# Reordering one tile's mixer: both channel halves of four projections ahead of the long convolution, the channel norm split by token half

## What is computed

```python
def mixer_block(u, ...):
    z = u @ w_in                                   # u = rms_norm(x)
    b_a, c_a, h_a, v_b, g_b = split(z)             # 512 channels each
    y_a = b_a * causal_dwconv(c_a * h_a, conv_a_w)             # 3 taps
    glu = v_b * sigmoid(g_b)
    cb = causal_dwconv(glu, conv_b_w) + conv_b_bias            # 31 taps
    y_b = silu(layer_norm(cb, ln_b_g, ln_b_b))                 # norm over 512 channels
    return concat([y_a, y_b]) @ w_out
for l in range(2):
    h = h + mixer_block(rms_norm(h), ...)
    h = h + memory_cross_attention(rms_norm(h), rms_norm(mem), ...)   # 4 heads, 256 memory tokens
    h = h + relu(rms_norm(h) @ w_up) ** 2 @ w_down                    # width 4096
return rms_norm(h)
```

## Time and profile before

| what | value |
|---|---|
| median of 3 runs | 3471.89 us (3469.18 to 3646.47) |
| the profiled execution | 3468.78 us, of which the span of the slowest core is 3467.2 us |
| spans of the eight cores | 3442.4 to 3467.2 us, granted clock 0.981 to 0.987 |
| busy share of the span | PE 94%, DVE 51%, ACT 40%, POOL 19% |
| PE idle ahead of L450 matmuls | 126.3 us |
| PE idle ahead of L906 matmuls | 58.9 us |

### The profile page before, as it was taken

How to read it: one execution, slowest core, us unless ns; L and a number is a source line. 1 busy time by engine, 2 the same in 40 slices (tenths; PEclk the granted TensorE clock), 3 DMA queues, 4 the chain that set the end, 5 groups by cost and what they waited for, 6 DMA issues and landing times.

```text
span 3467.2 us, 50455 instructions; the slowest of 8 cores (3442.4 to 3467.2 us)
## 1 busy us (share of the span) xinstructions
PE 3257.5 (94%) x16080; PEld 1550.2 (45%) x16080; DVE 1762.9 (51%) x2912; ACT 1402.1 (40%) x2627; POOL 643.7 (19%) x884
## 2 busy tenths in 40 slices
PE   2879999999998999989998999999999899999997
PEld 0445444444454444544444444444445444454443
DVE  4846333663357532564347743376335753366433
ACT  3336322463325531464333732256333553146421
POOL 0413001320032100330004200222003210042000
PEclk9989999999999999999999999999999999999999
DMA  7686944544555444535548344344456444453441
GB/s 202 150 187 102 166 73 85 118 91 79 110 167 124 80 78 82 122 79 86 98 94 228 64 80 76 91 113 83 77 117 177 111 80 79 75 127 72 77 80 52
DMA packets 132275, 366.93 MB, mean 106 GB/s; under 512 B 13872, under 2 KB 39728, under 8 KB 132016
## 3 DMA queue, kind: packets, MB, share of 16 engines
q0 software_dynamic: 59648, 213.94, 36.5%
q1 hardware_dynamic: 63152, 145.56, 13.3%
q10 hardware_dynamic: 9216, 4.20, 0.5%
HBM read 521.98 MB, written 34.60 MB: 161 GB/s over the span
## 4 chain that ended last, share of the span: by engine, by line
PE 83%; DVE 4%; issue 4%; DMA 3%; ACT 3%; POOL 1%; SPq 1%; DVEq 0%; ACTq 0%; POOLq 0%
PE ps L450 81%; ACT arena L461 3%; DMA arena<-wts 2%; DVE arena L465 2%; PE ps L906 2%; DVE arena L475 1%; DMA wbf<-arena 1%; SPq L577 1%; POOL arena L465 1%; DVE arena L610 0%; POOL arena L479 0%; POOL arena L470 0%; POOL arena L766 0%; DVE arena L951 0%; SPq L589 0%
## 5 line engine op out<-in xcount | busy, mean ns | idle before, releaser
L450 PE MATMUL ps<-arena 128*128 128x512 bf16 (+2 forms) x15816 | 3182.7, 364 | 126.3 <-ACT arena L461 64.9
L450 PEld LDWEIGHTS ps<-arena 128*128 128x128 bf16 x15816 | 1520.8, 98 | 1785.8 <-issue 175.6
L461 ACT ACTIVATE arena<-arena 128x512 bf16<-128x512 f32 (+3 forms) x1249 | 740.6, 642 | 1265.2 <-DVE arena L465 949.3
L465 DVE TENSOR_TENSOR arena<-arena 128x512 bf16<-128x512 f32 (+3 forms) x1200 | 849.5, 715 | 653.6 <-ACT arena L461 632.2
L465 DVE TENSOR_TENSOR arena<-ps,arena 128x512 f32<-128x512 f32 (+1 forms) x448 | 303.2, 688 | 633.7 <-PE ps L450 594.4
L461 ACT ACTIVATE arena<-ps 128x512 f32<-128x512 f32 (+1 forms) x608 | 361.8, 595 | 623.0 <-PE ps L450 599.2
L416 POOL DMA_DIRECT2D arena<-wts x400 | 214.7, 538 | 1662.6 <-PE ps L450 1621.1
L465 POOL TENSOR_TENSOR arena<-arena 128x512 f32<-128x512 f32 (+1 forms) x144 | 206.7, 1439 | 609.3 <-ACT arena L461 366.0
L461 ACT ACTIVATE arena<-ps,arena 128x256 f32<-128x256 f32 (+2 forms) x441 | 228.6, 533 | 135.9 <-DVE arena L471 72.9
L465 DVE TENSOR_TENSOR arena<-arena,ps 128x512 f32<-128x512 f32 x256 | 172.8, 686 | 141.2 <-PE ps L906 81.6
L475 DVE SCALAR_TENSOR_TENSOR arena<-arena 128x384 f32<-128x384 f32 (+3 forms) x336 | 179.3, 586 | 92.0 <-ACT arena L461 91.5
(11 more groups left out here) (14 smaller groups left out, 96.9 us busy)
## 6 DMA issues: line engine op xcount, KB each, us to landing
arena<-wts POOLq DMA_DIRECT2D x400, 512.0 KB, 5.9
arena<-wbf SPq DMA_DIRECT2D x64, 576.0 KB, 4.0
arena<-wbf SPq DMA_DIRECT2D x64, 512.0 KB, 5.4
arena<-xT SPq DMA_DIRECT2D x32, 512.0 KB, 6.8
outT<-arena SPq DMA_DIRECT2D x8, 2048.0 KB, 7.1
arena<-xT SPq DMA_DIRECT2D x6, 2048.0 KB, 15.6
wbf<-arena SPq DMA_DIRECT2D x16, 576.0 KB, 3.7
arena<-arena SPq DMA_DIRECT2D x128, 64.0 KB, 3.5
```

The lines of the kernel that those rows point to most:

```text
L450: ins = e.matmul(ps.ap, lhsT=l_, rhs=r_, start=(first and i == 0), stop=(last and i == n - 1))
L461: return e.activation(**kw)
L465: S.op(eng, lambda e: e.tensor_tensor(out=out.ap, in0=a.ap, in1=b.ap, op=op), reads=[a, b], writes=[out])
```

## The change

1. Order in `mixer`: g and v of channel half 0, c and h of half 0, g and v of half 1, layout transfers of `glu`, c and h of half 1, the convolution, then all eight b groups, token half by token half. `cva` has eight buffers instead of four. The weight order `seq` follows.
2. The channel norm runs per token half: for each s, DVE subtractions and multiplications of 4 x 128 columns (none on POOL now), four Silu of 128 columns per block, and per block again two transfers from SP and two from ACT, now of 256 bytes per row instead of 512. So there are 32 Silu of 128 columns, and 32 transfers, per mixer, instead of 16 of 256 columns, and 16 transfers.
3. `await_ln(s)` replaces `finish_tasks()` at the end of the mixer: the code goes on to `attend` and asks for half s of the norm where it is read. `out_half` takes six output blocks instead of four and goes block by block, y_a inputs first.
4. `next_ps` rotates over seven banks, `next_aux` has one.
5. Strided regions are given to the scheduler piece by piece (`ivs`), so that the two token halves of `ycat`, `cb` and `yb` don't wait for each other.
6. `conv_a`'s copy of the history into `c` is issued by POOL ahead of the h group.
7. The last tile's final norm is written out in pieces of two channel blocks (`final_last`).

```diff
@@ Buf
     def r3(self, j0, j1, a=0, b=None):
...
-        return self.ref(ap, j0 * self.stride + a, (j1 - 1) * self.stride + b)
+        return self.refs(ap, [(j * self.stride + a, j * self.stride + b) for j in range(j0, j1)])
...
-        cva = [alloc(T, F32, TAU) for _ in range(4)]
+        cva = [alloc(T, F32, TAU) for _ in range(8)]
...
         def next_ps():
-            return psref(rot("ps", range(6)))
+            return psref(rot("ps", range(7)))
         def next_aux():
-            return psref(6 + rot("aux", range(2)))
+            return psref(7)
...
                 for jp in range(2):
-                    seq += [w_id(l, C_G + jp), w_id(l, C_V + jp)]
-                seq += [w_id(l, C_C), w_id(l, C_H)]
+                    seq += [w_id(l, C_G + jp), w_id(l, C_V + jp), w_id(l, C_C + jp), w_id(l, C_H + jp)]
                 seq += [b_id(l, W_CONV + i) for i in range(8)]
-                seq += [w_id(l, C_B), w_id(l, C_C + 1), w_id(l, C_H + 1), w_id(l, C_B + 1)]
+                seq += [w_id(l, C_B), w_id(l, C_B + 1)]
@@ mixer
+            gv_part(0)
+            ch_part(0)
+            gv_part(1)
             touch(AF.Ln)
             copy("pool", glc.r3(0, NG, 0, HM), gluh[l].r3(0, NG))
...
+            ch_part(1)
...
+                        c = rot("chb", chb)
+                        hh = chh[l].r(2 * j, 2 * j + 2)
+                        h3 = Ref(hh.ap.unsqueeze(2), "sb", hh.lo, hh.hi)
                         psc = grp(sc, jj, xg, s)
                         t = tmp()
                         tt("dve", t.r(), psc, RB[s].r(), ALU.mult)
+                        copy("pool", c.r3(2, 4, 0, 1), h3)
                         psh = grp(sh, jj, xg, s)
-                        c = rot("chb", chb)
                         tt("dve", c.r3(0, 4, 1, TAU + 1), ps4(psh), p4(t), ALU.mult)
-                        spawn(conv_a(s, j, c, cva[s * 2 + jj]))
+                        copy("pool", h3, c.r3(2, 4, TAU, TAU + 1))
+                        spawn(conv_a(s, j, c, cva[s * 4 + j]))
@@ ln_task
-                yield
-                for a in range(5):
-                    if a < 4:
-                        blk = cb.r3(4 * a, 4 * a + 4)
-                        tt("dve", blk, blk, bc(ln_m), ALU.subtract)
-                        tt("pool" if a % 2 else "dve", blk, blk, bc(ln_v), ALU.mult)
-                    if a > 0:
-                        silu_out(a - 1)
+                for s in range(NS):
+                    blks = [cb.r3(4 * a, 4 * a + 4, s * TAU, (s + 1) * TAU) for a in range(4)]
+                    for a in range(2):
+                        tt("dve", blks[a], blks[a], bc(ln_m, s), ALU.subtract)
                     yield
+                    for a in range(4):
+                        if a < 2:
+                            tt("dve", blks[a + 2], blks[a + 2], bc(ln_m, s), ALU.subtract)
+                        tt("dve", blks[a], blks[a], bc(ln_v, s), ALU.mult)
+                        silu_out(a, s)
+                        yield
+                    ln_done.add(s)
                     yield
                 touch(AF.Ln)
...
             spawn(ln_task())
-            b_part(0)
-            ch_part(1)
-            b_part(1)
-            finish_tasks()
-            drain_bg()
+            sb_ = [ring_get(w_id(l, C_B)), ring_get(w_id(l, C_B + 1))]
+            for s in range(NS):
+                for j in range(4):
+                    psb = grp(sb_[j // 2], j % 2, xg, s)
+                    tt("dve", phased(ycat, j, s), ps4(psb), p4(cva[s * 4 + j]), ALU.mult)
+            ring_free(2)
             bgwork()
@@ attend
+                    if kh:
+                        await_ln(s)
+                    for ps, m in zip(pss, ms):
+                        tick()
+                        w3 = wk(ok[m // 2], 256)
+                        mm(ps, [(w3[:, k, (m % 2) * 128:(m % 2 + 1) * 128], rs[k].ap) for k in range(4 * kh, 4 * kh + 4)],
+                           [ok[m // 2].r(0, 2048)] + rs[4 * kh:4 * kh + 4], first=(kh == 0), last=(kh == 1))
+                        if kh:
+                            spawn(resid_task(s, m, ps, vb + V_X, rmo[s]))
...
-            out_half(0, (0, 1, 2, 3))
-            for m in range(4, 8):
+            out_half(0, (0, 1, 2, 3, 4, 5))
+            for m in range(6, 8):
                 O(0, m)
```

124 lines of the change are left out of this document (61 added, 63 removed).

## The result

The changed kernel is slower. It took 3545.91 and 3547.39 us, against 3469.18 and 3471.89 us before: the ratio is 1.0219, with a 95% interval from 1.0175 to 1.0263. The prediction was 3486 us with a range from 3443 to 3517. The profiles before and after are each of the slowest core of the chip, and these are two different cores.

What follows compares the result with a forecast made beforehand. PE, busy 94% of the span, was taken as the bound, with ACT setting the scores. Terms summed as 3468.8 + 19 - 6 + 4 - 1 = 3484.8, stated as 3486 us, range 3443 to 3517.

Steps and rivals of the forecast that it cites:

- The scores after 41.8 us: Each mixer, norm's sums to first score group: ACT sets it at 41.8 us, 3.4 us later than 38.4.
- The three waits: PE's waits per mixer: y_b inputs of s = 0, 5 us; those of s = 1, 4; scores, 5.
- the 52.1: Kernel before, one mixer: 52.1 us from the norm's sums to the scores, half clock after the 7.81 us wait included.
- The clock, +1.0: PE's half clock around the wait ahead of the scores: +1.0 us per mixer, between nothing and 2.9.
- Ahead of the sums, -1.65 per mixer: PE's idle time before the norm's sums, 1.65 us average, all regained through early history copy and earlier b weights.
- The single bank, +4: At three tile borders the second norm sum waits for ACT to read the first, near 1.3 us each: +4 us.
- The first mixer, -6: Loads bound the first mixer, the norm hides behind `setup(0)`, and two float32 loads leave the saturated stretch: -6 us.
- A: Norm hides: ACT issues beside Silu, scores at 30.5 us, total 3399, chance 0.05; milder form 3449, chance 0.16.
- B: ACT's long queue costs more: blocks of 3.6 us, +7 us per mixer, total 3515; chance 0.12.
- C: Change does nothing: same ACT work in another order, gain ahead of the sums pays; 3462 to 3480 us, chance 0.22.
- The three terms of -11.6, -6 and +4 us: Idle time ahead of norm's sums in seven mixers, -11.6; loads in the first mixer, -6; one sums bank at borders, +4.
- three signs of being wrong: Norm blocks at 2.5 us or less; ACT's block passes between them; PE's waits under 10 us per mixer.

Runs made afterwards that it cites:

- the gate on loads: Changed kernel with only the first six ring slots loaded at the start, the rest after layer 0's last `conv_build`: span 3542.4 us, ratio 1.0222.
- the best version: Changed kernel with POOL issuing ACT's norm transfers, six rotating and two sum banks, `h` load put off 14 ticks on SP: span 3423.0 us, ratio 0.9869.

## Why the prediction was wrong

**The scores after 41.8 us: right.** Found 42.2. The block of 3.15 us, eight of them, the table load behind them and the passes in a row came as worked out; so did four Silu at 1.65. By the price that the Trainium skill gives for an ACTIVATE (ScalarE: Activation LUTs, What ACT_TABLE_LOAD costs) they were estimated at 1.64 us, and the trace's 1.65 agrees. The three waits were put at 5, 4 and 5 us and were 3.8, 2.2 and 4.0 in the mixer shown, less in sum, because PE's own groups ran partly at a granted clock of 0.87 and 0.74 between them. The stall that was forecast in place of the old one came.

**The clock, +1.0: too small.** The stretch from the scores to the attention's output groups lasts 78.7 us instead of 76.3, +2.4 per mixer. The prediction gave the bounds as 0 and 2.9, and chose the lower half; the half clock cost 2.6 us behind the third wait, and what it had cost before was already in the 52.1. With the scores at +3.4 forecast and +4.1 found, this is the difference between 31 and 45.6 us.

**Ahead of the sums, -1.65 per mixer: the failed step.** The reasoning looked at the b weights and at `conv_a`, and both did improve (weights from 27.7 to 6.4 us of waits). But the prediction did not count what the layout transfers are moved past on SP's queue: it put a credit of 1.65 us in each mixer and no term at all for the 2 MB load of the next `h`. In the second-layer mixers (the last three; the first of them is counted with the start) the stretch came out at -0.2 us; in the three behind a tile border at +8.2 each (2.88 of it the single bank). The runs that moved the load show the cause: with it behind the layout transfers the wait is gone on all cores, and 25 us with it. Nor did the prediction look at POOL's queue, in which the eight layout issues now stand ahead of the history copies (4.80 us of DVE); with them on ACT one execution was about 10 us shorter.

**The single bank, +4: too small by half.** A wait of 1.3 us was put where 2.88 came, at each of three borders.

**The first mixer, -6: wrong in sign, +9.5.** The claim that the norm hides there behind `setup(0)` overlooked that ACT serves both, in the order of the program. PE waited 13.79 us for copies behind the norm's blocks. Taking the copies off ACT gave 3.6 us in that stretch, taking the issues off ACT 8 us. 7.4 of the 9.5 us already arise ahead of the first sums; 5.5 of these are longer waits at the memory norm (L653, 13.1 us; 7.6 before), of which two banks took away 3.3. The first groups behind 55 us start 4 us later, because DVE waits 4.9 us for the stores of the built weights, against 0.6; the gate on loads took this away and gained only 1.4.

**The rivals.** A (the norm hides) is refuted for the changed kernel, since issue and Silu never overlap on ACT. As a mechanism it is confirmed by the kernel whose issues stand on POOL: it forecast a block of 1.74 us and the scores at 30.5, and 1.57 us (with a pause of 2.27 us for DVE between the token halves) and 31.5 were found. B (ACT's queue costs more) named the right engine, but put the additional price into the blocks, which held at 3.15; it came from the clock and from the places that the prediction had given to the credit side. Its 3515 us is also summed wrongly: 7.0 at the scores, less 1.65 and plus 1.0, is 6.35 per mixer and gives 3510. C (nothing changes) is refuted by the 77 us. The three terms of -11.6, -6 and +4 us had no bounds of their own: the range held only the bounds of ACT's block. None of the three signs of being wrong that the prediction named came either, since all three looked only at the norm, ACT and the waits around it.

## What to carry to other kernels

Price a DMA issue on the engine that issues it, per transfer and not per byte: splitting a transfer in two doubles the issue time on the engine, and if that engine also does the arithmetic of the chain, the whole chain waits (here 16 issues of 0.66 us between the Silu of each of eight mixers cost 88 us of 3544). When a step is moved, write down for each queue (also SP's, also that of background work laid out by ticks) what now stands ahead of it; in this kernel a 2 MB load ahead of small transfers cost their consumer 6 to 9 us at each border of the slowest core, and moved out of one consumer's way it twice stood in the next one's (that of the b weights, that of the norm's transfers). Side work hides behind other work only if no engine serves both in program order. And where a change has seven points, try the cheapest one alone in the old kernel: here the history copy, one moved line, gave 22 us of the 44 that the best version gained.

## What the runs showed of the hardware

- The issue of two transfers takes 1.24 to 1.65 us on ACT, and no row of ACT's own work overlaps it; on POOL, idle at that time, two took 1.1 us. The transfers landed later with the issues on POOL, a median of 4.1 us (SP) and 3.8 (POOL) against 2.1, and it still paid. Whether they are late because the issues come closer together or because other loads run beside them wasn't separated.
- Half the bytes per transfer did not halve the landing: a median of 2.1 us for 32 KB in pieces of 256 bytes, against 2.5 us for 64 KB in pieces of 512 in the same order of work (the norm whole again) and 3.2 us in the kernel before.
- The same 2 MB load at the same border landed in 10.1 us with little beside it, in 12.2 beside the layout transfers and weight loads, in 23.4 in the kernel before beside ten weight loads, and in 32.9 on POOL's queue behind weight loads.
- The waits cost twice here: 10 us of waits in three pieces were followed by 5.2 us at 1.2 GHz, and in the kernel with the issues on POOL, with waits of 2.96 and 0.24 us, the same groups ran at a granted clock of 1.00.
